# Four groups of matmul operands moved by 32 to 256 bytes in SBUF: the distance to the weights modulo 512

## What is computed

```python
# first network, layer 0: a conformer convolution, then a gated MLP with a width-3 convolution
mod = silu(c) @ mod_w[l] + mod_b[l]                      # 6 x 1024 shifts, scales, gates, one row
u = h @ cm_w1 + cm_b1; u = a * sigmoid(gt); u = causal_dwconv(u, dw, dwb)   # 31 taps
y = silu(layer_norm(u)) @ cm_w2 + cm_b2
u = causal_dwconv(h @ w_in, dw, dwb); y = (silu(g) * v) @ w_out             # 1024 -> 2*2816 -> 1024
# layer 1: differential attention (h @ w_v, @ w_k, @ w_q, @ w_o), then the same MLP
# second network, layer 0: RWKV-7 time mixing (k, r, v, low-rank products, a scan, w_o), SwiGLU MLP
# layer 1: spatial gating unit (w_in, a 128x128 product per group, w_out), SwiGLU MLP
```

## Time and profile before

| | us |
|---|---|
| median of three runs | 1429.78 |
| the three runs | 1428.01, 1429.78, 1442.5 |
| the profiled execution | 1427.87 |
| its span, first to last instruction | 1426.0 |
| TensorE busy with matmuls | 1378.5 (97%) |
| TensorE busy with weight loads | 1309.1 (92%) |
| VectorE busy | 1047.9 (73%) |
| ScalarE busy | 734.9 (52%) |
| GpSimd busy | 217.6 (15%) |

### The profile page before, as it was taken

One profiled execution on the slowest core, in us unless ns is written; L12 is line 12 of the kernel. 1 busy time (PEld: TensorE's weight loads), 2 busy tenths in 40 slices (PEclk: granted clock), 3 DMA queues, 4 the chain that ended last, 5 costly groups with the idle time before them and its releaser, 6 DMA issues.

```text
span 1426.0 us, 31047 instructions
## 1 busy us (share of the span) xinstructions
PE 1378.5 (97%) x11806; PEld 1309.1 (92%) x11806; DVE 1047.9 (73%) x1636; ACT 734.9 (52%) x1193; POOL 217.6 (15%) x232
## 2 busy tenths in 40 slices
PE   8999999999988999999999999999999999999997
PEld 6998899999986899999888888799999998999997
DVE  6988799987996788883687965677774556677743
ACT  4547565645357556664366542553444447544442
POOL 0000133310000113321000010123330000133300
PEclk9999999999999999999999999999999999999999
DMA  9874367797881436665432400346666443466662
GB/s 376 304 254 174 123 224 238 258 388 261 312 305 48 162 119 192 191 223 189 162 104 74 120 17 2 101 136 188 184 208 202 146 119 119 139 201 194 211 203 70
DMA packets 68431, 258.16 MB, mean 181 GB/s; under 512 B 7545, under 2 KB 9857, under 8 KB 67970
## 3 DMA queue, kind: packets, MB, share of 16 engines
q1 hardware_dynamic: 68354, 257.10, 54.1%
HBM read 256.01 MB, written 1.06 MB: 180 GB/s over the span
## 4 chain that ended last, share of the span: by engine, by line
PE 80%; DVE 14%; ACT 3%; issue 2%; DMA 1%; DVEq 0%; ACTq 0%
PE ps L725 20%; PE ps L727 20%; PE ps L726 20%; DVE lo L1817 3%; PE ps L742 3%; DVE modraw L1823 2%; PE ps L686 2%; PE ps L688 1%; PE ps L687 1%; ACT hi L1297 1%; DMA modraw<-in_wmod 1%; DVE U L2378 1%; DVE products L2376 1%; PE ps L749 1%; DVE Y L1876 1%
## 5 line engine op out<-in xcount | busy, mean ns | idle before, releaser
L1817 DVE TENSOR_TENSOR lo<-raw,hi 128x1024 fp32r<-128x1024 f32 (+1 forms) x350 | 475.6, 1375 | 172.0 <-ACT hi L1297 171.4
L725 PE MATMUL ps<-OH,lo 128*128 128x256 f32 x1984 | 557.5, 281 | 4.5 <-DVE lo L1817 4.1
L726 PE MATMUL ps<-OL,hi 128*128 128x256 f32 x1984 | 551.8, 278 | 0.0
L727 PE MATMUL ps<-OH,hi 128*128 128x256 f32 x1984 | 551.8, 278 | 0.0
L1297 ACT ACTIVATE hi<-raw 128x1024 fp32r<-128x1024 f32 (+1 forms) x350 | 380.7, 1112 | 15.5 <-DMA raw<-in_w 9.3
L725 PEld LDWEIGHTS ps<-OH,lo 128*128 128x128 f32 x1984 | 373.8, 188 | 10.4 <-DVE lo L1817 7.7
L726 PEld LDWEIGHTS ps<-OL,hi 128*128 128x128 f32 x1984 | 374.2, 189 | 0.0
L727 PEld LDWEIGHTS ps<-OH,hi 128*128 128x128 f32 x1984 | 372.7, 188 | 0.0
L727 PE MATMUL ps<-GH,hi 128*128 128x256 f32 x704 | 196.1, 279 | 0.0
L725 PE MATMUL ps<-GH,lo 128*128 128x256 f32 x704 | 196.1, 278 | 0.0
L726 PE MATMUL ps<-GL,hi 128*128 128x256 f32 x704 | 196.1, 278 | 0.0
(11 more groups left out here) (382 smaller groups left out, 1951.2 us busy)
## 6 DMA issues: line engine op xcount, KB each, us to landing
raw<-in_w SPq DMA_DIRECT2D x288, 512.0 KB, 3.8
raw<-in_w SPq DMA_DIRECT2D x64, 704.0 KB, 5.0
modraw<-in_wmod SPq DMA_DIRECT2D x77, 512.0 KB, 5.5
modlate<-in_wmod SPq DMA_DIRECT2D x6, 512.0 KB, 5.0
modlast<-in_wmod SPq DMA_DIRECT2D x5, 512.0 KB, 4.8
modfirst_a<-in_wmod SPq DMA_DIRECT2D x4, 512.0 KB, 11.5
modfirst_b<-in_wmod SPq DMA_DIRECT2D x4, 512.0 KB, 12.0
l<-in_lora_in SPq DMA_DIRECT2D x1, 1536.0 KB, 6.3
```

The costliest lines, as they stand in the source:

```text
L725: pe.matmul(bank[:, 0:T], lo[:, r, w], oh[:, k0 + k], start=first, stop=False)
L726: pe.matmul(bank[:, 0:T], hi[:, r, w], ol[:, k0 + k], start=False, stop=False)
L727: ins = pe.matmul(bank[:, 0:T], hi[:, r, w], oh[:, k0 + k], start=False, stop=final)
L1817: dve.tensor_tensor(lo[:, s, 0:kt * P], raw[:, s, 0:kt * P], hi[:, s, 0:kt * P].bitcast(F32), ALU.subtract).then_inc(lo_made, 1)
```

## The change

Only the addresses of the eight input tiles change. `OH` and `OL` move up by 32 bytes, to 224 past the weights modulo 512. `GH` and `GL` move down by 32, to 160. `PH` and `PL` move down by 96, to 96. `RH2` and `RL2` move down by 256, to 448. No instruction is added, removed or moved in its engine's order; sizes, waits and transfers stay. All old addresses and the weights' are multiples of 64. Of the new ones, those of `RH2` and `RL2` are, and the other six are odd multiples of 32.

```diff
-        OH = at(2, "OH", [P, DC, T], F32R)
-        OL = at(2, "OL", [P, DC, T], F32R, plus=OPERAND)
+        OH = at(2, "OH", [P, DC, T], F32R, plus=32)
+        OL = at(2, "OL", [P, DC, T], F32R, plus=32 + OPERAND)
         tmp = at(4, "tmp", [P, 4, 2, T])
-        GH = at(5, "GH", [P, FC, T], F32R, plus=PHASE)
-        GL = at(5, "GL", [P, FC, T], F32R, plus=PHASE + 4 * FC * T)
+        GH = at(5, "GH", [P, FC, T], F32R, plus=PHASE - 32)
+        GL = at(5, "GL", [P, FC, T], F32R, plus=PHASE - 32 + 4 * FC * T)
@@
-        PH = at(5, "PH", [P, DC, T], F32R, plus=PHASE)
-        PL = at(5, "PL", [P, DC, T], F32R, plus=PHASE + OPERAND)
+        PH = at(5, "PH", [P, DC, T], F32R, plus=32)
+        PL = at(5, "PL", [P, DC, T], F32R, plus=32 + OPERAND)
@@
-        RH2 = at(4, "RH2", [P, DC, T], F32R, plus=2 * PHASE)
-        RL2 = at(4, "RL2", [P, DC, T], F32R, plus=2 * PHASE + OPERAND)
+        RH2 = at(4, "RH2", [P, DC, T], F32R)
+        RL2 = at(4, "RL2", [P, DC, T], F32R, plus=OPERAND)
```

## The result

The changed kernel takes 1451.26 us, the median of four runs (1450.39 to 1452.95). The kernel before, in its runs beside it, takes 1434.62 (four runs, 1428.01 to 1442.5). The ratio is 1.0133, with a 95% interval of 1.0086 to 1.018. It is slower, by 1.3% (by 1.2% if one median is divided by the other). The profiled execution took 1450.39 us with a span of 1448.5, 22.5 us more than before. Its granted clock is 0.995, as before.

A forecast was written before the change was run, and what follows sets the result against it. TensorE's matmul pitch was taken as the bound. Savings of 5.8, 7.0 and 4.5 us made 17.3, less 1.2 for transfers and 2.0 after hold-ups: 14.1 us off 1427.87, forecast 1414 us, range 1392 to 1449.

The forecast's parts named there:

- What bounds the kernel, and the two pitches: Large products: TensorE's rate sets the time; 113.3 and 117.8 ns a matmul hold themselves, selected anew by each hold-up.
- The step that failed: OH, OL at 224 and GH, GL at 160: slow pitch no longer holds, giving 5.8 us in ffn0, 7.0 in glu0.
- The terms of the sum: Savings of 5.8 us in ffn0, 7.0 in glu0 and 4.5 in the short phases, together 17.3 us.
- a mark against multiples of 64: Transform table, 128 from its weights: nine matmuls at 117.8 ns, short evidence that multiples of 64 can be slow.
- the slow pitch everywhere: Rival, chance 0.25: fast stretches vanish in ffn1, glu1 and elsewhere, 22.9 us less some hold-ups, about 1449 us.
- a third pitch: Slow rival's higher pitch: one more step of 4.45 ns would bring 40 us, 1489; no row had it.
- GH at 160 and OH at 224 differ: Sign of a wrong forecast: under a third pitch, down and up phases may differ from each other; no size given.
- PH and RH2 counted at nothing: Query and receptance phases, 192 matmuls each: each could move 0.9 us either way; no gain or loss counted.
- Writers in the middle of a 64-byte piece counted at nothing: VectorE and GpSimd writing the moved operands: extra cost hides under TensorE, exposed at most a microsecond; counted at nothing.
- Transfers and VectorE as the next bounds: ffn0_down's DMA share would reach 0.996, 1.2 us left out; VectorE would begin to bound ffn0_up at half a step.
- The base: Whole kernel before: forecast starts from the profiled 1427.87 us; the 1442.5 run hinted at ffn1 and glu1 turning slow.
- The rule of two independent read ports: TensorE's moving operand and weights have separate ports; by it no distance matters and the change is worth 0.

The follow-up runs named there:

- The small kernels: Three kernels of loop-form matmuls alone, no reference computed, varying input-to-weight distance, entry waits and disturbing matmuls; pitches from 111.7 to 122.3 ns a matmul.
- The map: Blocks of 48 loop-form matmuls in a kernel of their own, distances 0 to 480 bytes in steps of 32; 113.3 ns at 192, 120.0 at 0 and 96 modulo 256.

## Why the prediction was wrong

- **What bounds the kernel, and the two pitches**: right. TensorE's pitch is the bound, 113.3 and 117.8 both hold themselves at one distance, and a hold-up can leave either. The small kernels and the extra matmuls show each of these. One reading was too strong: of the 80% of the chain that TensorE has, the page gives the three lines of the loop 60, not nearly all.
- **The step that failed** is the first of the sum, "if the slow pitch no longer holds itself at these distances". I took 117.8 as the disturbance and 113.3 as the normal case, so that moving away from 192 could only cure. The map shows the reverse. 113.3 is the exception, found at 192 and rarely at 64 (modulo 256), and every other distance tried runs at 116.7 or more. The terms of the sum were sized well (ffn0 5.8, glu0 7.0 and the short phases 4.5 us, where 6.0, 7.0 and 4.3 us over 113.33 were there), but in place of giving back 17.3 us the new distances added 26.2. Moving away removed the good pattern, not the bad one. The two pitches that I saw were both of 192; I had one pair of rows at another distance, at 128, and those never reached 113.3. It was the only evidence on distances. I read it as a mark against multiples of 64; it spoke as well for every distance but 192 being slow, and I gave that too little weight.
- **The rival that came nearest**, the slow pitch everywhere, had the right places (ffn1 and glu1, 14.1 us) and one right argument, that 113.3 had been seen at 192 only. Its cause, half a 64-byte piece, was wrong: the whole multiples 0 and 256 are at 120.0, and input and weights that both begin inside such a piece are at 113.3. Its price was made with 117.8. The measured pitches are 118.33 on OH (6,528 x 0.55 ns = 3.6 us more), 117.4 to 118.7 on GH, and 120.0 on PH, 2.2 ns more over 192 matmuls, 0.4 us. So pitch added 26.2 us where the rival had 22.9 in all, and that is most of why 1451.3 lies 2.3 us above the range's end. That the profiled execution grew by 22.5 us, nearly the rival's 22.9, is luck: 2.7 us less of hold-ups made up for most of the third pitch. I had written that a third pitch was possible and left it out of the range.
- **GH at 160 and OH at 224 differ**, which the prediction named as a sign of a third pitch: 118.7 or 117.4 against 118.3.
- **PH and RH2 counted at nothing**: the query phase lost 1.0 us of pitch, the receptance phase nothing, since 448 is 192 plus 256.
- **Writers in the middle of a 64-byte piece counted at nothing**: right, by the kernel moved up as a whole (ratio 1.0) and by the busy times of the page. (GpSimd's largest share is in ffn1_up, 40.6 of 108 us, not the 28 of 80 that I gave; nothing hangs on it.)
- **Transfers and VectorE as the next bounds**: not reached. In the kernel with OH alone at 224, ffn0_down ran at 113.3 (55 us for 485.6 matmuls) with the DMA engines busy for 0.98.
- **The base**: the profiled execution, 1427.87, was one with two MLPs in the good pattern. In further runs the kernel before had medians of 1429.6 to 1441.7. The 1442.5 that I read as ffn1 and glu1 turning has no trace. It fits the kernel moved up as a whole, whose profiled execution took 1442.11 with ffn1, glu0 and glu1 at 117.8.
- **The rule of two independent read ports** (Trainium skill, SBUF — State Buffer, section Who interferes with whom): these runs don't agree with what I took from it, that the distance can't matter. With everything else equal, the distance alone moves the pitch from 113.3 to 120.0, and the kernel at 256 takes 1.7% more than at 192. The measurement decides. The 262 cycles for 256 columns of the Trainium skill (TensorE: Matmul & The Clock Gate, section Back-to-back issue gap), 109.2 ns by estimate, were not reached even with an input that walks no memory (111.7).

What stays open is the mechanism in the memory. Why the good pattern exists at 192 modulo 256 and not four bytes beside it, and why 0, 96, 184 and 200 are at 120.0 and 196 above that, isn't explained by any run. That two streams meet is the reading that fits: the pitch falls to 111.7 when one of them stands still. It is argued and not shown. No whole kernel was run at distance 64, where one block of seven reached 113.3, nor one that pairs another distance with extra matmuls of other lengths.

## What to carry to other kernels

When one loop shows two rates at a full clock and no idle time, ask first which of the two is the exception: a single run of a small kernel that goes through all distances tells in a millisecond what the rates of one distance can't, if each distance is entered often enough to see rare patterns too. A kernel whose runs spread by a per cent may be switching between two patterns of its main loop, and a cheap extra matmul behind the last hold-up can hold the good one; here it brought 0.9% and cut the spread to a third. Compare address changes by their pitch in each phase, not by a run's total, which also holds the luck of the selection.

## What the runs showed of the hardware

- At full clock, a stream of 128 x 128 float32r weight tiles with 256 moving columns has a pitch of 111.7 ns with an input that is one column, 113.3 at best with one that is walked, and up to 122.3, by the distance in bytes between input and weights. It repeats every 256 bytes (seen for steps of 32), and moving both sides by 32 bytes changes nothing.
- At distance 192 modulo 256 there are two stable pitches, 113.3 and 117.8. Waits of slightly different lengths led to them in 11 and 13 of 24 cases, and one and the same length led now to one and now to the other. Four bytes from 192 neither is found.
- One float32 matmul of 32 columns turned 7 of 7 blocks from 117.8 to 113.3, one of 128 columns 1 of 6; a float32r one of 16 columns turned 5 of 5 the other way. In the whole kernel it also turned 4 of 11 stretches of ffn0 from 117.8 to 113.3. An extra float32 matmul in such a stream costs 0.23 us, 0.09 of it in the matmul behind it.
